# Latent attention in pairs of heads, V as the stationary operand in two column halves, probabilities scaled before they are transposed

## The reference

```python
qh  = (rms_norm(mq, ...) @ mla_w_q_up).reshape(B, S, 8, 64 + 32)      # 64 plain, 32 rotary columns
kvh = (rms_norm(mkv, ...) @ mla_w_kv_up).reshape(B, S, 8, 64 + 64)    # 64 of K, 64 of V
q = concat(qh[..., :64], rope(qh[..., 64:])); k = concat(kvh[..., :64], rope(mkr) for every head)
s = einsum('bqhd,bkhd->bhqk', q_blk, k) * 96 ** -0.5                  # query blocks of 128
s = where(k_chunk <= q_chunk, s, min)                                 # chunks of 64: chunk-causal
p = softmax(s);  out = einsum('bhqk,bkhe->bqhe', p, v)
```

## Time and profile before

| | us |
|---|---|
| median of 3 runs (1942.32 to 1943.52) | 1942.8 |
| the profiled execution | 1942.39 |
| its span | 1940.6 |
| PE busy | 1908.9 (98%), 12792 matmuls |
| DVE busy | 1225.4 (63%) |
| ACT busy | 792.0 (41%) |
| POOL busy | 637.2 (33%) |

### The profile page before, as it was taken

How to read it: one execution, slowest core, us unless ns; L and a number is a source line. 1 busy time by engine, 2 the same in 40 slices (tenths; PEclk the granted TensorE clock), 3 DMA queues, 4 the chain that set the end, 5 groups by cost and what they waited for, 6 DMA issues and landing times.

```text
span 1940.6 us, 31226 instructions
## 1 busy us (share of the span) xinstructions
PE 1908.9 (98%) x12792; PEld 1711.4 (88%) x12792; DVE 1225.4 (63%) x1631; ACT 792.0 (41%) x1148; POOL 637.2 (33%) x490
## 2 busy tenths in 40 slices
PE   7999999999999999999999999999999999999998
PEld 6999988897668999998899999889966789999886
DVE  5888843534555788872578888344354467888523
ACT  5344433334454444442443444232344544444322
POOL 3566500002230566620045664000022325666000
PEclk9999999999999999999999999999999999999999
DMA  4233233321003123323312333332200122222321
GB/s 164 88 109 108 103 121 125 102 100 44 1 23 130 46 108 108 108 109 131 130 44 88 108 108 109 130 131 95 86 22 3 64 87 88 106 93 105 127 101 66
DMA packets 27370, 180.43 MB, mean 93 GB/s; under 512 B 3298, under 2 KB 3460, under 8 KB 7300
## 3 DMA queue, kind: packets, MB, share of 16 engines
q1 hardware_dynamic: 25760, 174.15, 25.1%
q10 hardware_dynamic: 1508, 4.87, 0.8%
HBM read 176.91 MB, written 2.10 MB: 92 GB/s over the span
## 4 chain that ended last, share of the span: by engine, by line
PE 95%; ACT 1%; DVE 1%; issue 1%; DMA 0%; SPq 0%; POOLq 0%; POOL 0%; DVEq 0%; ACTq 0%
PE ps L461 27%; PE ps L463 27%; PE ps L462 27%; PE ps L811 2%; PE ps L700 1%; PE ps L829 1%; PE ps L473 1%; PE ps L621 1%; PE ps L623 1%; PE ps L622 1%; PE ps L709 1%; PE ps L818 1%; PE ps L762 0%; PE ps L756 0%; DMA raw<-stream 0%
## 5 line engine op out<-in xcount | busy, mean ns | idle before, releaser
L461 PE MATMUL ps<-xH,WH 128*128 128x256 f32 (+2 forms) x1424 | 427.5, 300 | 3.0 <-DVE xL L1314 3.0
L463 PE MATMUL ps<-xH,WL 128*128 128x256 f32 (+2 forms) x1424 | 424.9, 298 | 0.0
L462 PE MATMUL ps<-xL,WH 128*128 128x256 f32 (+2 forms) x1424 | 424.9, 298 | 0.0
L462 PE MATMUL ps<-TL,WH 128*128 128x256 f32 x1216 | 344.5, 283 | 0.0
L463 PE MATMUL ps<-TH,WL 128*128 128x256 f32 x1216 | 344.5, 283 | 0.0
L461 PE MATMUL ps<-TH,WH 128*128 128x256 f32 x1216 | 344.5, 283 | 0.0
L1265 DVE TENSOR_TENSOR WL<-raw,WH 128x2048 fp32r<-128x2048 f32 x62 | 143.0, 2307 | 264.4 <-ACT WH L925 249.5
L461 PEld LDWEIGHTS ps<-xH,WH 128*128 128x128 f32 (+1 forms) x1424 | 273.4, 192 | 11.8 <-issue 4.3
L462 PEld LDWEIGHTS ps<-xL,WH 128*128 128x128 f32 (+1 forms) x1424 | 273.3, 192 | 8.5 <-issue 1.0
L463 PEld LDWEIGHTS ps<-xH,WL 128*128 128x128 f32 (+1 forms) x1424 | 273.3, 192 | 7.6
L461 PEld LDWEIGHTS ps<-TH,WH 128*128 128x128 f32 x1216 | 233.6, 192 | 0.0
(11 more groups left out here) (249 smaller groups left out, 3655.1 us busy)
## 6 DMA issues: line engine op xcount, KB each, us to landing
raw<-stream SPq DMA_DIRECT2D x156, 1024.0 KB, 4.8
norm_g<-norm_gains SPq DMA_DIRECT2D x12, 512.0 KB, 5.3
x<-x_in SPq DMA_DIRECT2D x4, 512.0 KB, 8.1
wq<-w_q_up ACTq DMA_DIRECT2D x4, 512.0 KB
out<-x SPq DMA_DIRECT2D x4, 512.0 KB, 2.7
const<-consts ACTq DMA_DIRECT2D x2, 578.5 KB
wkv<-w_kv_up ACTq DMA_DIRECT2D x2, 512.0 KB
cos<-positions ACTq DMA_DIRECT2D x2, 256.0 KB
```

The source lines that it names most:

```text
L461: mm(dst, wh, xh, start=start, stop=False)
L462: mm(dst, wh, xl, start=False, stop=False)
L463: return mm(dst, wl, xh, start=False, stop=stop)
```

## The change

It touches the latent attention of both layers alone.

- **Order.** Heads are taken in pairs and, within a pair, block by block from the widest to the narrowest: step m is head 2 * (m // 8) + m % 2 and block 3 - m % 8 // 2.
- **Scaling.** The division by the row sum moves: DVE's `scale(m)` takes the reciprocal of one sum and multiplies the probabilities in place, up to 512 columns, before they are transposed; `turn(m)` waits for it. It is issued at the start of DVE's step m - 2, one place behind `tops(m)`. `shares` and `keep_head` go.
- **Values.** `values(p)` runs once for two steps, with V as the stationary operand (128 x 64) and the probabilities of a block as 128 moving columns. The even head writes PSUM rows 0 to 63, the odd head rows 64 to 127, in turn. The result is already transposed, so `turn_heads` goes, and `keep_heads` and `low_heads` read the output bank itself.
- **K.** One product makes K of two heads (128 rows) and is then copied in two halves. Odd heads hold their rotary rows in the lower half, so the rotary key is made for all 128 rows and copied once for each of four buffers, two of these from buffer to buffer on ACT at n = 1 and n = 3. The host packs the weights to fit.
- **Buffers and waits.** Four q and k buffers and three for the transposed probabilities, the further ones in space that is free in this stage. `turn_q(h)` on DVE now also waits for `keep_q(h)` on ACT. `make_q` stands at steps 0 and 4 of eight, `make_k` at step 2.

```diff
+def head_and_block(m):
+    return m // 8 * 2 + m % 2, BLK - 1 - m % 8 // 2
...
+        q_of = (qT[:, 0, :], qT[:, 1, :], acc[:], q_spare[:])
+        k_of = (kT[:, 0, :], kT[:, 1, :], sin[:], zg[:])
+        p_of = (probT[:, 0, :], probT[:, 1, :], ks_ret[:])
...
-                    def make_k(h):
-                        pe.wait_ge(q_kept, due(q_kept, h + 1))
-                        pe.wait_ge(q_ready, due(q_ready, h + 1))
-                        at = h * (NOPE + DV)
-                        mm(ps[0:NOPE, QK_BANK, :], wkv[:, at:at + NOPE], ckv[:], start=True, stop=True).then_inc(k_psum, 1)
+                    def make_k(i):
+                        pe.wait_ge(q_kept, due(q_kept, 2 * i + 1))
+                        pe.wait_ge(q_ready, due(q_ready, 2 * i + 1))
+                        mm(ps[:, QK_BANK, :], wkv[:, 2 * i * NOPE:(2 * i + 2) * NOPE],
+                           ckv[:], start=True, stop=True).then_inc(k_psum, 1)
...
                     def turn(m):
-                        pe.wait_ge(exped, due(exped, m + 1))
-                        for kk in range(m % BLK + 1):
+                        pe.wait_ge(scaled, due(scaled, m + 1))
+                        for kk in range(head_and_block(m)[1] + 1):
...
-                        for kk in range(b + 1):
-                            last = mm(ps[:, OUT_BANK, b * DV:(b + 1) * DV], probT[:, m % 2, kk * P:(kk + 1) * P],
-                                      v_mla[:, kk, h * DV:(h + 1) * DV], start=kk == 0, stop=kk == b)
+                    def values(p):
+                        h, b = head_and_block(2 * p)
+                        pe.wait_ge(turn_kept, due(turn_kept, 2 * p + 2))
+                        if b == BLK - 1 and h:
+                            pe.wait_ge(headsL_ready, due(headsL_ready, h // 2))
+                        for kk in range(b + 1):
+                            for e in range(2):
+                                last = mm(ps[e * DV:(e + 1) * DV, OUT_BANK, b * P:(b + 1) * P],
+                                          v_mla[:, kk, (h + e) * DV:(h + e + 1) * DV],
+                                          p_of[(2 * p + e) % 3][:, kk * P:(kk + 1) * P], start=kk == 0, stop=kk == b)
...
                     for n in range(STEPS):                      # PE
-                        h, b = divmod(n, BLK)
+                        i = n // 8 + 1
                         turn(n)
-                        if n:
-                            values(n - 1)
-                        if h + 2 < HEADS and b == 1:
-                            make_q(h + 2)
-                        if h + 2 < HEADS and b == 2:
-                            make_k(h + 2)
-                        if h and h % 2 == 0 and b == 3:
-                            turn_heads(h // 2 - 1, QK_BANK)
+                        if n and n % 2 == 0:
+                            values(n // 2 - 1)
+                        if i < HEADS // 2:
+                            if n % 8 == 0:
+                                make_q(2 * i)
+                            elif n % 8 == 2:
+                                make_k(i)
+                            elif n % 8 == 4:
+                                make_q(2 * i + 1)
                         linear(n)
                         if n + AHEAD < STEPS:
                             scores(n + AHEAD)
...
                     for n in range(STEPS):                      # ACT
                         keep_turn(n)
+                        if n and n % 8 == 0:
+                            keep_heads(i - 2)
+                        if i < HEADS // 2:
+                            if n % 8 == 0:
+                                keep_q(2 * i)
+                            elif n % 8 == 2:
+                                keep_k(i)
+                            elif n % 8 == 4:
+                                keep_q(2 * i + 1)
+                        if n in (1, 3):
+                            ...
+                            af(k_of[j + 2][r, :], k_of[j][r, :], ACT.Copy).then_inc(kpe_copied, 1)
                         linear(n)
...
                     def turn_q(h):                              # DVE
                         dve.wait_ge(q_psum, due(q_psum, h + 1))
...
+                        dve.wait_ge(q_kept, due(q_kept, h + 1))
+                        r = rope_rows(h)
+                        tt(q_of[h % 4][r, :], ps[r, QK_BANK, :], cos[r, :], ALU.mult).then_inc(q_ready, 1)
...
+                    def scale(m):
+                        width = (head_and_block(m)[1] + 1) * P
+                        dve.wait_ge(exped, due(exped, m + 1))
+                        link(nc.vector.reciprocal(share[:, 0, m % 4:m % 4 + 1], total[:, 0, m % 4:m % 4 + 1]))
+                        ts(prob[:, m % 3, 0:width], prob[:, m % 3, 0:width], share[:, 0, m % 4:m % 4 + 1], None,
+                           ALU.mult).then_inc(scaled, 1)
...
                     for m in range(AHEAD):
                         tops(m)
+                    scale(0)
+                    scale(1)
                     for n in range(STEPS):
-                        h, b = divmod(n, BLK)
-                        if h and b == 0:
-                            keep_head(h - 1)
-                        if b == 2:
-                            shares(h)
-                        if h and h % 2 == 0 and b == 3:
-                            low_heads(h // 2 - 1, QK_BANK)
-                        if h + 2 < HEADS and b == 1:
-                            turn_q(h + 2)
+                        i = n // 8 + 1
+                        if n + 2 < STEPS:
+                            scale(n + 2)
+                        if n % 8 == 1 and n > 8:
+                            low_heads(i - 2)
+                        if i < HEADS // 2 and n % 8 in (0, 4):
+                            turn_q(2 * i + n % 8 // 4)
                         linear(n)
                         if n + AHEAD < STEPS:
                             tops(n + AHEAD)
```

More of the change, by code:

```diff
@@ L834, in mixed @@
                         return [(xH[:, 2 * i + a, :], xL[:, 2 * i + a, :]) for a in range(2)]
-                    def turn_heads(i, bank):
-                        pe.wait_ge(head_kept, due(head_kept, 2 * i + 2))
-                        if bank == QK_BANK:
-                            pe.wait_ge(k_kept, due(k_kept, min(2 * i + 5, HEADS)))
-                        for b in range(BLK):
-                            last = nc.tensor.transpose(ps[:, bank, b * P:(b + 1) * P], pair_out[i % 2][:, b, :], ident[:])
-                        last.then_inc(heads_turned, 1)
                     make_values(2)
@@ L855, in mixer @@
                     pe.wait_ge(kpe_ready, due(kpe_ready, 1))
-                    mm(ps[NOPE:P, LIN_BANKS[0], :], twice[NOPE:QK, :], krgg[NOPE:QK, :], start=True,
+                    mm(ps[:, LIN_BANKS[0], :], twice[NOPE:QK, :], krgg[NOPE:QK, :], start=True,
                        stop=True).then_inc(kpe_psum, 1)
@@ L863, in mixer @@
                     scores(0)
-                    make_k(1)
                     scores(1)
@@ L1145, in keep_q, with keep_k @@
                         act.wait_ge(q_psum, due(q_psum, h + 1))
-                        if h >= 2:
-                            act.wait_ge(scored, due(scored, (h - 1) * BLK))
-                        af(qT[0:NOPE, h % 2, :], ps[0:NOPE, QK_BANK, :], ACT.Copy).then_inc(q_kept, 1)
-                    def keep_k(h):
-                        act.wait_ge(k_psum, due(k_psum, h + 1))
-                        af(kT[0:NOPE, h % 2, :], ps[0:NOPE, QK_BANK, :], ACT.Copy).then_inc(k_kept, 1)
+                        if h >= 4:
+                            act.wait_ge(scored, due(scored, (h // 2 - 1) * 8))
+                        r = nope_rows(h)
+                        af(q_of[h % 4][r, :], ps[r, QK_BANK, :], ACT.Copy).then_inc(q_kept, 1)
+                    def keep_k(i):
+                        act.wait_ge(k_psum, due(k_psum, i + 1))
+                        if i >= 2:
+                            act.wait_ge(scored, due(scored, (i - 1) * 8))
+                        for h in (2 * i, 2 * i + 1):
+                            r = nope_rows(h)
+                            af(k_of[h % 4][r, :], ps[r, QK_BANK, :], ACT.Copy).then_inc(k_kept, 1)
                     def exps(m):
-                        width = (m % BLK + 1) * P
+                        width = (head_and_block(m)[1] + 1) * P
                         act.wait_ge(top_ready, due(top_ready, m + 1))
@@ L1234, in mixer @@
                             exps(n + AHEAD)
-                    keep_heads(HEADS // 2 - 1, OUT_BANK)
+                    keep_heads(HEADS // 2 - 1)
                     for i, slot in ((10, 4), (11, 5)):
@@ L1676, in mixer @@
                             tops(n + AHEAD)
-                    keep_head(HEADS - 1)
-                    low_heads(HEADS // 2 - 1, OUT_BANK)
+                    low_heads(HEADS // 2 - 1)
                     for i in range(2, OUT_PAIRS):
@@ L1862, in pack @@
```

(5 more changed lines are left out.)

114 lines of the change are left out of this document (52 added, 62 removed).

## The result

The changed kernel took 1963.23 us (median of 4 runs, 1961.18 to 1964.14) beside 1943.16 us for the kernel before on the same chip: a ratio of 1.0099, with a 95% interval of 1.0081 to 1.0116. It is slower by about 20 us. The forecast was 1946.8 us with a range of 1930 to 1962, so the time lies just outside the range. The direction of the likeliest case was right and its size was not.

What follows compares the result with a forecast made beforehand. PE bounded the loop before; scale, maxima and exponential in series on DVE and ACT would set its pace after. 2.0 us more in each of two layers, +4.0 on 1942.39, plus 0.4 for the median: 1946.8 us, range 1930 to 1962.

Steps and rivals of the forecast that it cites:

- the series: In the attention loop, scale, row maxima and exponential follow one another on DVE and ACT, mean period 2.02 us; chance 0.62.
- The rival in which PE stays the bound: In the loop, DVE's scale and waits overlap better than walked, so PE sets the pace: 1918 us; chance 0.13.
- The rival of halves that don't overlap: Value products on the two column halves don't overlap, 7.2 us of PE a layer come back: 1951.6 us; chance 0.10.
- The reading that the spread's rows leave no gap: The norms' spread on PE, between full-width products, shows no gap, against a drain rule worth 3 us a layer.
- the saving of the value products: On PE in the loop, 160 value records at 0.064 us each instead of about 0.12: 8.8 us less a layer.
- what PE loses: PE's work in the loop falls by 14.3 us a layer: values 8.8, K 3.7, turned heads 1.8.
- the first rival: The rival in which PE stays the bound of the loop: 1918 us; chance 0.13.
- The series without waits: DVE's gap from the third to the last exponential with no waits: 57.7 + 6.2 + 17.3 = 81.2 us a layer.
- The waits of the walk: DVE's waits found by walking the loop's 32 steps: 14.2 us a layer, of these turn_q 7.2, scores 4.4, masked copy 2.0.
- the rival of TensorE's clock: PE's idle time in the loop brings more time at the lower clock: +6 us a layer, 1958.8 us; chance 0.15.
- The tail: After the loop's last exponential: 4.2 us to the last value product at 589.9, with five tiles to 596.9.
- Outside the two loops every stage should have its old length: A check on the sum: no stage outside the two layers' loops changes length, else a place was left out.

Runs made afterwards that it cites:

- e3: The kernel before with only the in-place scaling of the probabilities added at the start of DVE's step: 1956.27 us, ratio 1.0071.
- e10: e5 with scale(0) put between the row maxima of blocks 1 and 2 and scale(1) left to follow later: 1934.79 us, ratio 0.9961.
- e8: The changed kernel without reciprocal and product (output left undivided), and with turn_q not waiting for keep_q: 1933.87 us, ratio 0.9961.
- e7: The changed kernel with eight unused transposes on PE ahead of the turn at steps 0 and 23 to 29 (filler): 1959.63 us, ratio 1.0093.
- e5: The changed kernel with scale(n + 2) behind tops(n + 3) and turn_q not waiting for keep_q: 1938.75 us, ratio 0.9981.
- e6: e5 with the blocks of a pair in rising order of width, not falling: 1938.60 us, ratio 0.9983.
- e1: The changed kernel with scale(n + 2) on DVE moved behind tops(n + 3), nothing else: 1950.55 us, ratio 1.0039.
- e4: The changed kernel with turn_q on DVE no longer waiting for keep_q on ACT: 1956.97 us, ratio 1.0066.
- e9: The changed kernel with low_heads put ahead of scale(n + 2) at the steps that begin a pair: 1958.10 us, ratio 1.0086.

## Why the prediction was right and wrong

**Right: the series sets the pace.** DVE waits 28 times for the exponential, 0.53 to 0.85 us each, as the prediction asked for, and e3 shows that the product in this place lengthens the loop alone, by 7.4 us a layer. The rival in which PE stays the bound fell.

**Right: the halves overlap.** Sixteen value records pass in 1.03 us, 0.064 each. The rival of halves that don't overlap fell. The reading that the spread's rows leave no gap was wrong, though. Record by record the changed kernel shows one on each side of a group:

```profile
549.85 0.32 PE L848 MATMUL ps<-ks_ret,v_mla 128*64 128x128 f32 x1 [0.95 <-ACT probT L1181]
550.02 0.27 PE L848 MATMUL ps<-probT,v_mla 128*64 128x128 f32 x1
550.22 1.98 PE L713 MATMUL ps<-mq,wq 128*128 128x512 f32 x4
...
571.89 0.27 PE L836 MATMUL ps<-ident,prob 128*128 128x128 f32 x1
572.09 0.32 PE L848 MATMUL ps<-ks_ret,v_mla 128*64 128x128 f32 x1
```

Within a group a pair of records passes in 0.11 us (572.25, 572.36, 572.47), but the full-width product behind the last pair starts 0.20 after it (550.02 to 550.22). Three transposes ahead of full-width scores pass in 0.11 each (563.48 to 563.81), and one ahead of value products takes 0.20 (571.89 to 572.09). The rule on drains that the prediction cites (the Trainium skill, TensorEngine Tiling (Array Packing), Key Properties) thus agrees with this trace, at some 0.09 us ahead of and 0.09 behind each group. The 0.064 of the spread held both, spread over 16 records; the pace without them is 0.055. For the 16 groups of a layer, of 10 records on the mean, that makes the saving of the value products about 7.4 us for 8.8, an estimate from these rows.

**Too high: what PE loses.** The step had 14.3 us a layer. At a clock of 1.00 (e10) PE's busy time in the loop stretch is 10.1 us less than before (125.39 to 115.24), and part of that is the fall at the squares, which the kernel before has and e10 has not. The groups' two edges would explain 1.4 of the missing 4.2. It decided nothing in the changed kernel, since PE did not bound it, but it would have made the first rival's 1918 unreachable. So would the handshakes: without the product (e8) the loop falls only to 125.4 us.

**Where the 20 us are.** The gap between the third and the last exponential was forecast at 95.4 us, 81.2 of them without waits. DVE's table of waits splits the measured gaps the same way:

| | gap | waits | rest |
|---|---|---|---|
| forecast | 95.4 | 14.2 | 81.2 |
| changed, layer 1 | 102.8 | 19.5 | 83.3 |
| changed, layer 2 | 101.5 | 18.3 | 83.2 |
| filler, layer 1 (clock 1.00) | 98.1 | 14.9 | 83.2 |
| filler, layer 2 (clock 0.98) | 100.3 | 17.1 | 83.2 |

- The series without waits was mis-sized by 2.0 us a layer, 4 in all. Most of it is `scale`: over the 29 in the first layer's gap, reciprocal and product took 0.57 us from start to start on the mean, for 0.52, 1.3 us in all. A 512-wide block took 0.60 (577.81 to 578.41) for 0.62, but a 384-wide one whose successor is the mask 0.63 (580.78 to 581.41) for 0.55. The other 0.7 was not traced.
- The waits of the walk were nearly right at full clock: 14.9 for 14.2, with `turn_q` 8.0 for 7.2, scores 5.1 for 4.4 and the masked copy 1.6 for 2.0 (e7, first layer).
- **The step that failed** is the clock. The sum has no term for it, and "Against it: PE's waits are 1 to 2 us each" gave the rival of TensorE's clock 0.15. The ends of the exponentials show what it cost in its place: 4.75 us in the first loop's gap and 3.47 in the second's. At those places PE's work took up to 1.8 times its time (3.36 us for 1.88, 1.97 for 1.09), so a q or scores came late and DVE stood. The rival had it at 6 us a layer, and its sign, a granted clock under 0.95 over the loop, came true in the first loop (0.91) and was just missed in the second (0.95). The waits of 2.0 and 2.2 us are not the whole of it: the fall at the squares, 1.5 and 2.3 of these us, came in the first layer with PE busy for 9.97 of 10 us, and the earlier trace rows already showed such a fall. The walk took PE's work there at full clock. What makes the clock fall stays open.
- The tail from exp(31) to the end of five tiles was 12.2 us in the first layer for 11.2; in the second, to the last value product, 4.5 for 4.2.
- "Outside the two loops every stage should have its old length" failed by 1.6 us, and that is the clock too. The stretch between the loops was 827.4 or 827.5 us in before, e5, e6 and e8, 828.8 to 829.1 in the changed kernel, e1 to e4, e9 and e10, and 830.5 in e7, though no edit of the experiments lies there. The same 35 us of it, from 755 us behind its start, in the kernel before, the changed kernel and e7:

```profile
1368.98:1403.98 35.00, 35.00 (x269) 33.52 (x268) 10.03 (x11) 10.94 (x16) 1.65 (x1) 1.00 0.26 91
1379.23:1414.23 35.00, 35.00 (x260) 33.71 (x259) 9.84 (x10) 9.46 (x12) 1.65 (x1) 0.95 0.25 91
1374.70:1409.70 35.00, 35.00 (x247) 33.68 (x246) 9.88 (x10) 9.24 (x11) 1.65 (x1) 0.90 0.25 91
```

The clock there is 1.00 in all four kernels with the short stretch, 0.95 in all seven with the middle one and 0.90 in e7. PE is busy for all of the 35 us in each, so idle time is not what lowers it here. Why it falls in some kernels and not in others stays open.

Per layer the terms close. First: 2.1 + 5.3 (waits, with the clock) + 1.0 (tail) = 8.4, against the 8.5 by which 10.5 exceeds the forecast 2.0. Second: 2.0 + 4.1 + 0.3 = 6.4, against 8.4 − 2.0. With the 1.6 between the loops this is the 16 us that the forecast lacked. Of these some 10 are the clock (4.75, 3.47 and 1.6), 4 the series without waits, and the rest waits and tail. That the time came out only 1 us above the range is no credit to the sum: the range had room for most of that rival.

## What to carry to other kernels

An instruction put at the head of an in-order queue, right behind the one that feeds its producer, makes three engines take turns: the edit that moves it behind the next block's independent work (with the second wait of the same kind gone) turned a loss of 0.99% into a gain of 0.19%, with the same arithmetic. When a change lowers the load of the bounding engine, price the clock as well: where it fell here, the work took up to 1.8 times as long, and over half of the missed 16 us was that. Count the places that are at the lower level before the change too. And work taken from the bound is a gain only as far as the next handshakes let it be: here 10 us a layer were saved on PE, and 4.6 arrived in the best version. A repeated stretch at full clock is a good ruler: it separates what an edit does from where the clock happened to fall.

## What the runs showed of the hardware that was not expected

- The same idle stretch of 2.01 us on TensorE was followed by the lower clock in one layer and not in the other: 3.36 and 1.88 us for one product in the changed kernel. In e5 it is the second layer that falls; the first has the same wait at 489.27 and shows 1.00 from 484 to 494 us.
- The lower clock also came with TensorE busy throughout: 35.00 of 35 us between the loops, at 0.95 or 0.90 where other kernels have 1.00, for 1.6 or 3.1 us of time.
- A loop was shorter with more TensorE work: with 64 unused transposes, some 4 us, the first took 134.9 us for 139.5. How much of that the fillers did is shown for the loop's end only.
- Between full-width work and products on half of the columns some 0.09 us more pass than within either, in both directions.
- The in-place multiplication by a column took 506 ns on the mean at 512 columns, 452 at 384, 353 at 256 and 286 at 128: a quarter of the columns costs more than half of the time.
